# VectorE computes four modulation units in the first MLP's last group too, TensorE five units a group

## What is computed

```python
def adaln(cond, w, b):
    m = jax.nn.silu(cond) @ w + b
    m = m.reshape(cond.shape[0], 6, 1, D_MODEL)
    return [m[:, j] for j in range(6)]

def modulate(x, g, shift, scale):
    return rmsnorm(x, g) * (1 + scale) + shift

def sq_relu_mlp(h, w1, w2):
    return jnp.square(jax.nn.relu(h @ w1)) @ w2

# reference(), for the context stream; the latent stream has the same lines
mp = sq_relu_mlp(modulate(xp, norm_g[l, 2], sh2p, sc2p), w1_mlp[l], w2_mlp[l])
xp = xp + g2p * rmsnorm(mp, norm_g[l, 3])
```

## Time and profile before

| what | us |
|---|---|
| median of three runs (2488.64 to 2493.11) | 2492.58 |
| the profiled execution, its own time | 2489.31 |
| its span | 2487.5 |
| TensorE busy in the span | 2434.9 (98%) |
| VectorE busy | 1685.1 (68%) |
| ScalarE busy | 1087.3 (44%) |
| GpSimd busy | 262.6 (11%) |
| the first MLP's last group, from its first matmul to the end of n = 3 | 1112.35 to 1303.9 |

### The profile page before, as it was taken

The page is one execution under the profiler, slowest core; times in us unless marked ns, Lnnn a source line. Parts: engine busy times, 40 slices in busy tenths (PEclk is TensorE's granted clock), DMA queues, the critical chain, the costliest instruction groups (busy, mean ns, idle before and its releaser), DMA issues.

```text
span 2487.5 us, 37359 instructions
## 1 busy us (share of the span) xinstructions
PE 2434.9 (98%) x13794; PEld 1991.1 (80%) x13794; DVE 1685.1 (68%) x2118; ACT 1087.3 (44%) x1495; POOL 262.6 (11%) x465
## 2 busy tenths in 40 slices
PE   6899999999999999999999999999999999999998
PEld 3578888778888888888887877798888888888887
DVE  2246665587767767775568877675888678564665
ACT  3234443464333433333454456585644344343343
POOL 0021111000010010000012144200001001000000
PEclk8999999999999999999999999999999999999999
DMA  9999999969888988987877956659668668666564
GB/s 359 372 289 342 321 322 302 320 225 309 294 278 287 308 284 267 310 281 257 281 251 244 307 171 221 222 190 299 204 226 278 208 220 279 197 200 206 169 207 166
DMA packets 458056, 651.39 MB, mean 262 GB/s; under 512 B 21976, under 2 KB 316696, under 8 KB 456280
## 3 DMA queue, kind: packets, MB, share of 16 engines
q1 hardware_dynamic: 426272, 543.47, 65.6%
q0 software_dynamic: 29312, 105.12, 12.6%
q10 hardware_dynamic: 2360, 1.32, 0.2%
HBM read 634.39 MB, written 15.43 MB: 261 GB/s over the span
## 4 chain that ended last, share of the span: by engine, by line
PE 92%; DMA 3%; DVE 2%; ACT 1%; issue 1%; SPq 0%; DVEq 0%; ACTq 0%
PE PS L1380 24%; PE PS L1461 14%; PE PS L1462 14%; PE PS L1463 14%; PE PS L1383 12%; PE PS L1409 3%; DMA SCR<-in_w_ada 1%; DMA RAW<-in_w_o_na 1%; PE PS L1599 1%; PE PS L1391 1%; PE PS L1393 1%; PE PS L1392 1%; PE PS L1600 1%; PE PS L1601 1%; PE PS L1574 1%
## 5 line engine op out<-in xcount | busy, mean ns | idle before, releaser
L2002 DVE TENSOR_TENSOR WLO<-RAW,WHI 128x1024 fp32r<-128x1024 f32 x740 | 873.6, 1225 | 293.0 <-ACT WHI L1715 242.1
L1380 PE MATMUL PS<-HM,WHI 128*128 128x512 f32 x2560 | 648.4, 395 | 3.0 <-issue 2.6
L1715 ACT ACTIVATE WHI<-RAW 128x1024 fp32r<-128x1024 f32 x370 | 390.2, 1055 | 417.0 <-DMA RAW<-in_w_mlp 163.7
L1380 PEld LDWEIGHTS PS<-HM,WHI 128*128 128x128 f32 x2560 | 459.6, 189 | 101.8 <-issue 15.7
L1461 PE MATMUL PS<-WHI,HID 128*128 128x512 f32 x1152 | 450.5, 391 | 0.0
L1462 PE MATMUL PS<-WLO,HID 128*128 128x512 f32 x1152 | 448.4, 389 | 0.0
L1463 PE MATMUL PS<-WHI,HID 128*128 128x512 f32 x1152 | 448.2, 389 | 0.0
L1719 ACT ACTIVATE WHI<-RAW 128x1024 fp32r<-128x1024 f32 x370 | 388.7, 1051 | 97.4 <-DMA RAW<-in_w_mlp 65.4
L1383 PEld LDWEIGHTS PS<-HM,WLO 128*128 128x128 f32 x2560 | 348.9, 190 | 25.6
L1383 PE MATMUL PS<-HM,WLO 128*128 128x256 f32 x2560 | 356.5, 282 | 0.0
L2075 DVE SCALAR_TENSOR_TENSOR X<-X,CS 128x1024 f32<-128x1024 f32 x240 | 297.0, 1279 | 1.4 <-DMA X<-in_w_ada 0.4
(11 more groups left out here) (260 smaller groups left out, 1994.9 us busy)
## 6 DMA issues: line engine op xcount, KB each, us to landing
RAW<-in_w_mlp SPq DMA_DIRECT2D x512, 512.0 KB, 5.4
ADW<-in_w_ada SPq DMA_DIRECT2D x114, 1024.0 KB, 9.9
X<-in_w_ada POOLq DMA_DIRECT2D x224, 256.0 KB, 3.9
RAW<-in_w_qkv_na SPq DMA_DIRECT2D x68, 512.0 KB, 8.6
RAW<-in_w_qkvg_gla SPq DMA_DIRECT2D x64, 512.0 KB, 5.5
SCR<-in_w_ada SPq DMA_DIRECT2D x16, 1024.0 KB, 11.5
RAW<-in_w_o_na SPq DMA_DIRECT2D x32, 512.0 KB, 7.2
RAW<-in_w_qkvg_gla SPq DMA_DIRECT2D x64, 256.0 KB, 5.0
```

Of the source, the lines that this page charges most:

```text
L1380: return mm(bank[:, 0:2 * T2], hi[:, k, P * b:P * b + P], act[:, kc, 0:2 * T2], start=first, stop=False)
L1715: actv(WHI[:, 2 * s + u, 0:HALF], RAW[:, u, 0:HALF], ACT.Copy).then_inc(hi_half, 1)
L2002: tt(WLO[:, 2 * s + u, part], RAW[:, u, part], WHI[:, 2 * s + u, part].bitcast(f32), ALU.subtract).then_inc(done, 1)
```

## The change

VectorE makes a quad in all four groups of the first MLP (`QUADS0` goes from 3 to 4), and TensorE makes five units a group instead of six: the one behind x = 2 of n = 1 goes. In the last group the tiles stand closer: nine in the up-projection (`LAST_UP`), one in each slab and one behind the last, four in n = 0 and three in n = 1 (`LAST_TILES`), and `quad_rows` runs behind x = 3 of n = 1. Behind it X returns, during n = 2. ScalarE's squares of X move to n = 2 and 3 for it, and it stores the quad's rows in n = 2. GpSimd loads the gain of n = 0 and 1 before the last tile and that of n = 2 and 3 after X. In stages with a flush at n = 3 the row sum moves behind the first cross products.

```diff
-        PU = NB + 2
+        PU = NB + 1
-        QUADS0, QUADS1 = HID_GROUPS - 1, 2
+        QUADS0, QUADS1 = HID_GROUPS, 2
...
+            if f == 1:
+                parts = ("y0", "y1", "x0", "x1", "y2", "x2", "g0", "g1", "x3", "g2")
...
-        PLAN_MLP = ((0,), (1,), (), ())
+        PLAN_MLP = ((0,), (), (), ())
...
+        LAST_TILES = (4, 3, 0, 0)
+        LAST_UP = KC - sum(LAST_TILES)
...
             pool.wait_ge(hid_done, HID_GROUPS * KC + 2)
+            pool.wait_ge(quad_out, QV * (16 * QU) + 16)
             pool.dma_start(CB[:, 0:768], t_gla).then_inc(sem("gla_in"), 16)
...
-                    if quads is not None and n == YN - 1 and x == 3:
+                    if quads is not None and norm is None and n == YN - 1 and x == 3:
+                        quad_rows(g + quads, 2 * layer + 2)
+                    if quads is not None and norm is not None and n == 1 and x == 3:
+                        pe.wait_ge(mod_done, 3)
                         quad_rows(g + quads, 2 * layer + 2)
...
-            mlp(0, M_MLP0, A_MLP0, 2, 0, QUADS0, FROM0)
-            mlp_group(HID_GROUPS - 1, 0, M_MLP0, A_MLP0, 2, 1)
+            mlp(0, M_MLP0, A_MLP0, 2, 0, HID_GROUPS - 1, FROM0)
+            mlp_group(HID_GROUPS - 1, 0, M_MLP0, A_MLP0, 2, 1, FROM0)
+            pe.wait_ge(quad_row, QV + 1)
             turn_rest(2, output_base(M_MLP0))
...
+                if n == YN - 2 and f == 1:
+                    quad_store(QV - 1, QUAD_UNITS[QV - 1])
...
-                if 0 < n < YN - 1:
+                if 0 < n < YN - 1 and f != 1:
                     more_squares(f, (("x0",), ("x1",))[n - 1])
+                if n == YN - 2 and f == 1:
+                    more_squares(f, ("x0", "x1"))
...
+            def out_tiles(q):
+                return LAST_TILES if isinstance(q, int) and q == QV - 1 else OUT_TILES
...
-                quad_out_tile(quad, n, 0)
+                if quad is not None and out_tiles(quad)[n]:
+                    quad_out_tile(quad, n, 0)
...
-                if flush is not None:
+                if flush is not None and n < YN - 1:
                     sum_rows(flush)
...
                         for x in range(3):
+                            if x == 1 and flush is not None:
+                                sum_rows(flush)
                             for b in range(2):
                                 cross(f, x, b)
...
-                for x in range(1, OUT_TILES[n]):
-                    quad_out_tile(quad, n, x)
+                if quad is not None:
+                    for x in range(1, out_tiles(quad)[n]):
+                        quad_out_tile(quad, n, x)
...
+                elif complete:
+                    hidden_body(g, 0, layer, m, quad, (0, 1), 1)
+                    with dve.Fori(1, NB) as i:
+                        hidden_body(g, i, layer, m, quad, (0, 1), 1)
+                    quad_tile(quad, LAST_UP - 1, (LAST_UP - 1) % 2, NB)
...
-            def load_gain(f):
+            def load_gain(f, parts=range(YN)):
+                if 0 in parts:
...
-                for n in range(YN):
+                for n in parts:
...
             for q in range(FROM0, QV):
                 for k in range(KC):
+                    if q == QV - 1 and k == KC - 1:
+                        load_gain(1, (0, 1))
                     quad_load(q, k)
             return_x(QV)
-            load_gain(1)
+            load_gain(1, (2, 3))
```

More of the change, by code:

```diff
@@ L294, in build_program @@
         UP_TILES = KC - sum(OUT_TILES)
+        LAST_TILES = (4, 3, 0, 0)
+        LAST_UP = KC - sum(LAST_TILES)
+        assert LAST_UP == 2 * NB + 1
         QUAD_SLOT = [k % 2 for k in range(KC)]
@@ L1267, in with_between @@
                 at = YN - 1 if plan[YN - 2] else YN - 2
-                return plan[n] + ((max(map(max, filter(None, plan))) + 1,) if n == at else ())
+                return plan[n] + ((sum(map(len, plan)),) if n == at else ())
             for n in range(YN):
@@ L1273, in mlp_group, with unit_ada @@
             def mlp_group(g, layer, m, a, at, more=False):
-                def unit_ada(i, x, halves=range(2)):
+                def unit_ada(i, x, halves=range(2), skip=SKIP0):
                     if a is not None:
-                        load_ada(g * PU + i + (a + x), at, g * (GU * UC) + i * UC + ((a + x + SKIP0) * UC - at * ADA), halves)
+                        load_ada(g * PU + i + (a + x), at, g * (GU * UC) + i * UC + ((a + x + skip) * UC - at * ADA), halves)
                 with sp.Fori(0, NB) as i:
@@ L1288, in ada @@
                         if plan:
-                            unit_ada(0, NB + plan[0], halves)
+                            unit_ada(0, NB + plan[0], halves, SKIP0 if NB + plan[0] < PU else SKIP0 + QU)
                     load_out(g * (4 * NB) + (m + 2 * NB), n, w2_mlp[layer], g * D, ada)
@@ L1945, in mlp @@
                     mlp_group(g, layer, m, a, (g + (quads - 1), g * units + (QUAD_UNITS[quads] - units)))
-                mlp_group(HID_GROUPS - 1, layer, m, a, (QV - 1, QUAD_UNITS[QV - 1]) if layer == 0 else None, True,
+                mlp_group(HID_GROUPS - 1, layer, m, a, (QV - 2, QUAD_UNITS[QV - 2]) if layer == 0 else None, True,
                           layer == 1)
@@ L2076, in quad_tile @@
                 end.then_inc(quad_step, 1)
+            def out_tiles(q):
+                return LAST_TILES if isinstance(q, int) and q == QV - 1 else OUT_TILES
             def quad_out_tile(q, n, x):
                 if q is not None:
-                    k = UP_TILES + sum(OUT_TILES[:n]) + x
+                    k = KC - sum(out_tiles(q)[n:]) + x
                     quad_tile(q, k, QUAD_SLOT[k], QUAD_SLOT[:k].count(QUAD_SLOT[k]))
@@ L2318, in mlp @@
                 mlp_group(0, layer, m, False, first, False)
-                with dve.Fori(1, quads) as g:
+                with dve.Fori(1, min(quads, HID_GROUPS - 1)) as g:
                     mlp_group(g, layer, m, False, g + first)
@@ L2323, in mlp @@
                         mlp_group(g, layer, m)
-                mlp_group(HID_GROUPS - 1, layer, m, True)
+                mlp_group(HID_GROUPS - 1, layer, m, True, HID_GROUPS - 1 + first if quads == HID_GROUPS else None)
             def mlp_group(g, layer, m, complete=False, quad=None, add=True):
@@ L2337, in mlp_group, with hidden_body @@
                              complete and layer and n == YN - 1, quad=quad)
-            def hidden_body(g, i, layer, m, quad=None, tiles=()):
+            def hidden_body(g, i, layer, m, quad=None, tiles=(), ahead=0):
                 for s in range(2):
@@ L2345, in hidden_body @@
                     if s in tiles:
-                        quad_tile(quad, i * 2 + (s - 1), 1 - s, i + (s - 1))
+                        quad_tile(quad, i * 2 + (s - 1 + ahead), (1 + s + ahead) % 2, i + ((s + 1 + ahead) // 2 - 1))
                     for b in range(2):
@@ L2410, in _ @@
             pool.dma_start(FLIP, t_window[:, P:2 * P]).then_inc(sem("flip_in"), 16)
-            def load_gain(f):
-                pool.wait_ge(gain_row, f + 1)
-                pool.dma_start(gain_rows[f].rearrange("b (k n) -> k b n", k=KC), GAIN_ROW).then_inc(gain_stored, 16)
-                pool.wait_ge(gain_stored, 16 * (f + 1))
+            def load_gain(f, parts=range(YN)):
+                if 0 in parts:
+                    pool.wait_ge(gain_row, f + 1)
+                    pool.dma_start(gain_rows[f].rearrange("b (k n) -> k b n", k=KC), GAIN_ROW).then_inc(gain_stored, 16)
+                    pool.wait_ge(gain_stored, 16 * (f + 1))
                 m0 = (M_WO0, output_base(M_MLP0), M_WO1, output_base(M_MLP1))[f]
-                for n in range(YN):
+                for n in parts:
                     if n >= 2:
```

## The result

| | before | after |
|---|---|---|
| median of six runs, us | 2492.66 (2488.64 to 2493.91) | 2501.68 (2497.86 to 2503.06) |
| ratio, 95% interval | | 1.0038 (1.0026 to 1.0051) |
| span of the profiled run, us | 2487.5 | 2496.1 |
| mean granted clock | 0.996 | 0.991 |

The kernel is slower by 9.0 us. The forecast was 2493.0 in a range of 2483 to 2500: the time lies above the range, and the case that held (slower) had a chance of 0.23.

A forecast was written before the change was run, and what follows sets the result against it. TensorE, busy 98% of the span, was taken as the bound. Units -8.4, `quad_rows` +1.2, tile 12 +1.2, tile 15 +8.7, clock +2.3 and row sum -2.6 give +2.4 us: forecast 2493 us, range 2483 to 2500.

The forecast's parts named there:

- the case that held (slower): Outcome of a measurably slower kernel, chance 0.23; its main case was tile 15 landing late, 2496 to 2500 us.
- the forecast's 1257.0: Group 3, n = 1: trace time in us when GpSimd first asks for tile 15, behind the gain's store and four loads.
- The late tile 12: Group 3, n = 0: tile 12 waits for tile 10's slot, so TensorE waits 1.2 us at `turn_gain`.
- The clock: After TensorE's wait at the end of n = 1, work runs at the lower clock: +2.3 us, between 0 and 3.
- The moved row sum: Two other stages with a flush at n = 3: -2.3 us in the attention's output stage, together -2.6 (0 to -3.2).
- The 0.3 of the GLA stage: GLA stage: the row sum moved behind other VectorE work saves 0.3 us of a 0.70 us wait.
- the landing of tile 15: Group 3, n = 1: tile 15 lands 6.1 us after its request (3.3 to 9.0), so TensorE waits 8.7 us.
- Rival 2: Slower: tile 15 queues behind gains and weights, lands after 8 to 9 us; 2496 to 2500 us, chance 0.23.
- After that ... cost nothing: Behind n = 1: X's return during n = 2 takes 8.8 us and is free while it lands within about 11.
- Rival 1: Faster: tile 15 is not late for TensorE; with no wait 2480 to 2483 us; chance 0.17.
- Rival 3: The removed TensorE units were hidden behind something else, so the -8.4 us is lost: 2500 us, chance 0.03.

The follow-up runs named there:

- both edits: Changed kernel with tile 15 asked for ahead of the gain's store and loads, and ten tiles instead of nine ahead of n = 0: 2489.72 us, ratio 0.9992.

## Why the prediction was wrong

**What held.** TensorE is the bound, and work taken from it counts: groups 0 to 2 gave 6.28 us where three units were put at 6.27. The order in which GpSimd asks, and `store_gain`'s place, were read rightly: tile 15 asked for behind store and gains, some 1249.4, and the forecast's 1257.0, less the 7.0 us by which after is ahead at group 3's start, is 1250.0. The late tile 12 cost TensorE 1.54 us (forecast 1.2, bounds 0 to 2.5). The clock cost 1.9 us (forecast 2.3): from its first matmul to the next slab `quad_rows` took 1.86 instead of 1.00, and the stretch behind n = 2 is 1.1 us longer, its first matmul 0.80 instead of 0.39. The Trainium skill ("TensorE: Matmul & The Clock Gate", Part 1) has the gated clock as the state of an idle engine; the granted clock of 0.50 in the slices of the wait agrees. The moved row sum gave 2.1 us in the attention's stage (forecast 2.3), but not where it was put: the wait of 3.00 us fell only to 2.77, and two earlier waits of TensorE, 1.07 and 0.28 us, are gone. The 0.3 of the GLA stage did not come: from its row turn to the second MLP both profiles took 21.08 us.

**The step that failed** is the landing of tile 15, in the part on n = 1. It was put at 6.1 us, "nearest to the gains just ahead of it", with bounds from 3.3 to 9.0, the latter the kernel's slowest tile. It took 9.7 to 11.3, beyond the upper bound. With it the wait is 12.64 us instead of 8.7 (8.6 by the forecast's own times): 3.9 of the 6.2 us by which the sum, +2.4, falls short of the profile's +8.6; the 1.4 us that this execution lost before the change begins are the next term. The runs show two parts in its place. The four gains ahead add 3.0 us, 1.5 a pair (10.5, 9.0 and 7.5 us with four, two and none). And with none ahead the tile at that place still takes 7.5 us, not the 3.3 of the calmer stretch, 1.5 of it for the unit beside it; what makes up the rest is open. So 6.1 was below even the tile without gains, and nothing was added for those ahead. Landings of the gains and of the tile in before, added up, come to 9.0 to 11.2 and enclose the 10.5, but that is not how it came about: in after the tile's first half landed together with the last gain, at about 1259.1. Rival 2 had the mechanism (queues behind gains and weights) and the point of decision, 7.5 us, but stopped at 9. The sum's range was too narrow as well: its own bounds of wait, clock and moved sum, set end to end, run from -3.4 to +8.6, not to +7.

**A second step was wrong without showing.** "After that ... cost nothing": X's return in n = 2 was said to be free if it lands within 11 us. After lands it in 10.0 and the stretch is hardly longer, so it seems right; but without the wait it lands in 11.0 us, at the limit named, and costs 4 to 6 us, through weights that land late, which the forecast had not thought of; ScalarE's squares, which it had, stand in that path too, behind those weights and not behind X. Rival 1 ("faster", 2480 to 2483 if tile 15 is not late) is therefore wrong by about that amount: its condition was met with both edits, at 2489.7, and its time was all but reached, 2483.3, only where X's return was cut to an eighth.

**The other rivals.** Rival 3 falls with groups 0 to 2. That VectorE has no room for the tiles (B), which was not among them, is worth 3.4 us with nine tiles ahead of n = 0, and 0 to 1.1 in the four kernels with ten and the tile first whose X returns whole.

## What to carry to other kernels

A transfer's landing time holds for its place: the same 512 KB landed in 4.6 us with the tile first, in 7.5 with the gain's store ahead and the gain loads behind, and each pair of gain loads ahead added 1.5 more. A landing time from another place is no estimate for one that is moved behind other loads, and moving the request that is needed first to the front took back all of the loss here. When a wait is taken away, look at what the wait had been hiding; here a 2 MB transfer that was nearly free beside an idle TensorE cost 4 to 6 us once TensorE was no longer idle. And the smallest part of the change, the row sum moved behind work that waits for nothing, came out as low by itself (2489.7 us) as the whole change mended in two places (2489.7); both are only just at the edge of what these runs tell from the kernel before. The lowest median with nothing left out was 2488.5.

## What the hardware showed

- A 512 KB load in two halves landed in 3.5 to 5.6 us when it was asked for ahead of the gain's store, in 6.0 (unit later) to 7.5 with the gain row's store just ahead and 1 MB of gain loads right behind it, in 9.0 with half of them ahead and in 10.1 to 10.5 with all of them ahead (medians but for the first).
- SP's own issue of a load of weights, 0.37 us otherwise, took 5.51 and 3.14 us while X's 2 MB and the unit's were under way, 2.71 with an eighth of X, and at most 0.79 with all of X and the unit later. So a queue that only issues can itself be late; in the last case the last of these loads landed no sooner for it.
- A DMA share near 1 can go with very different rates: 0.94 to 0.99 with 264 to 278 GB/s while gains, tile and weights moved, and 1.02 with 310 to 382 where the unit moved too.
- Idles of TensorE between 2.4 and 3.0 us left the clock at 2.4 GHz in some executions and brought it to 1.2 GHz for a part of what followed in others, at the same place of the program.
